# The u projection of each prompt tile as two column halves of the TensorE array

## What is computed

```python
h = rms_norm(x, norm1_g)
proj = h @ w_in
z, xbc, dt_raw, gu, gv = jnp.split(proj, ...)      # 512, 1024, 8, 512, 512 columns
...                                                # Mamba-2 scan over xbc and dt, gated by silu(z)
gu = jax.nn.gelu(gu)
gv = layer_norm(jax.nn.gelu(gv), ln_v_g, ln_v_b)
mixed = jnp.einsum("hts,bcshd->bcthd", w_s, v) + b_spatial...
gmlp_out = gu * mixed
x = x + jnp.concatenate([ssd_out, gmlp_out], axis=-1) @ w_out
x = x + hier_moe(rms_norm(x, norm2_g), ...)        # top 1 of 4 groups, top 2 of 8 experts
```

## Time and profile before

| | before |
|---|---|
| times of 3 runs | 2911.25 to 2912.52 us, median 2912.45 |
| the profiled execution: its time / its span | 2912.39 / 2910.5 us |
| TensorE busy | 2859.1 us, 98% of the span |
| TensorE weight loads busy | 1890.8 us, 65% |
| VectorE, ScalarE, GpSimd busy | 1580.8, 806.9, 878.5 us |
| the chain that ended last | TensorE 96% |
| granted TensorE clock, mean | 0.992 |

### The profile page before, as it was taken

How to read it: one execution, slowest core, us unless ns; L and a number is a source line. 1 busy time by engine, 2 the same in 40 slices (tenths; PEclk the granted TensorE clock), 3 DMA queues, 4 the chain that set the end, 5 groups by cost and what they waited for, 6 DMA issues and landing times.

```text
span 2910.5 us, 38335 instructions
## 1 busy us (share of the span) xinstructions
PE 2859.1 (98%) x12809; PEld 1890.8 (65%) x12809; DVE 1580.8 (54%) x4163; ACT 806.9 (28%) x1517; POOL 878.5 (30%) x1366
## 2 busy tenths in 40 slices
PE   8999999999999999999999999989999999999997
PEld 6677777677767776777777677754444444444443
DVE  5565555655565655565555656564444444444444
ACT  1223322323232323223222323212222222222222
POOL 0121112111211111121112111214566565666665
PEclk9999999999999999999999999989999999999999
DMA  7221221112121212211121112257675667567653
GB/s 312 106 79 52 73 80 52 59 66 80 52 71 60 74 51 73 74 58 59 66 80 51 61 64 73 75 220 250 246 261 186 221 202 257 202 220 265 245 169 126
DMA packets 109623, 369.01 MB, mean 127 GB/s; under 512 B 39497, under 2 KB 41426, under 8 KB 99442
## 3 DMA queue, kind: packets, MB, share of 16 engines
q1 hardware_dynamic: 48946, 252.91, 23.9%
q0 software_dynamic: 60480, 113.57, 11.8%
HBM read 325.09 MB, written 140.33 MB: 160 GB/s over the span
## 4 chain that ended last, share of the span: by engine, by line
PE 96%; DVE 2%; DMA 1%; issue 0%; POOL 0%; SPq 0%; ACT 0%; POOLq 0%; DVEq 0%; ACTq 0%
PE PB L368 23%; PE PB L1581 19%; PE PB L379 16%; PE PB L463 12%; PE SS L1621 9%; PE YB L463 4%; PE TB L1566 2%; PE YB L417 2%; PE TB L357 1%; DMA arena<-in_w_in 1%; PE SS L426 1%; PE TB L440 1%; PE SS L430 1%; PE TB L404 1%; PE YB L1614 1%; PE MB L408 1%
## 5 line engine op out<-in xcount | busy, mean ns | idle before, releaser
L368 PE MATMUL PB<-arena,hT 128*128 128x512 f32 (+2 forms) x2112 | 726.2, 497 | 1.2 <-DVE arena L1108 0.9
L368 PEld LDWEIGHTS PB<-arena,hT 128*128 128x128 f32 x2112 | 398.2, 191 | 269.4 <-issue 222.0
L1581 PE MATMUL PB<-arena,hT 128*128 x1296 | 569.3, 592 | 0.0
L379 PE MATMUL PB<-hT,arena 128*128 128x128 f32 x4224 | 487.8, 277 | 4.3 <-DVE arena L1096 4.3
L379 PEld LDWEIGHTS PB<-hT,arena 128*128 128x128 f32 x4224 | 482.3, 193 | 8.2 <-issue 4.6
L1581 PEld LDWEIGHTS PB<-arena,hT 128*128 128x128 f32 x1296 | 246.1, 190 | 309.7 <-issue 309.7
L1133 POOL TENSOR_SCALAR rs<-sq 128x2 f32<-128x2 f32 (+1 forms) x66 | 14.1, 214 | 1299.5 <-ACT h L732 960.8
L463 PE MATMUL PB<-arena,tT 128*128 128x274 f32 (+1 forms) x1056 | 358.7, 494 | 0.7 <-ACT tT L636 0.7
L1621 PE MATMUL SS<-arena,xdt 128*128 x640 | 287.9, 592 | 0.0
L463 PEld LDWEIGHTS PB<-arena,tT 128*128 128x128 f32 x1056 | 196.0, 190 | 141.3 <-issue 121.1
L795 DVE SCALAR_TENSOR_TENSOR xc<-xT,cols,xc 128x128 f32<-128x128 f32 x792 | 216.8, 346 | 3.5
(11 more groups left out here) (273 smaller groups left out, 3598.0 us busy)
## 6 DMA issues: line engine op xcount, KB each, us to landing
arena<-in_w_expert SPq DMA_DIRECT2D x32, 2048.0 KB, 8.8
arena<-in_w_expert SPq DMA_DIRECT2D x32, 1024.0 KB, 6.4
h_rows<-h SPq DMA_DIRECT2D x34, 512.0 KB, 2.7
x_in<-in_x_rows SPq DMA_DIRECT2D x33, 512.0 KB, 4.6
hT<-in_x_cols SPq DMA_DIRECT2D x33, 512.0 KB, 3.7
x_res<-in_x_rows SPq DMA_DIRECT2D x33, 512.0 KB, 5.1
dec<-running_sums SPq DMA_DIRECT2D x33, 512.0 KB, 3.6
first_rows<-bc SPq DMA_DIRECT2D x33, 512.0 KB, 4.0
```

Source lines behind the costliest of these rows:

```text
L368: mm = nc.tensor.matmul(out, hT[u][:, k, :], w_group(name)[:, k, :], start=k == 0, stop=k == KD - 1)
L379: mm = nc.tensor.matmul(PB[b][:, c * P:(c + 1) * P], w_block(name, c)[:, k, :], hT[u][:, k, :], start=k == 0, stop=k == KD - 1)
L1581: mm = nc.tensor.matmul(PB[u][:, :], hT[u][:, k, :], arena[:, bass.ds(slot + k * 2 * DE, 2 * DE)], start=k == 0, stop=k == KD - 1)
```

## The change

The u projection of the 32 tiles that `pe_turn` projects (tiles 1 to 32, the sample tile among them) is given as two matmuls for each `k`. One has the tokens 0 to 63 as its stationary operand and writes partitions 0 to 63 of `PB[0]`, the other has tokens 64 to 127 and partitions 64 to 127. Both have the same 512 moving columns of weights. Tile 0, projected in `pe_phase1`, stays as it was. The waits and the one semaphore increment, on the last matmul, stay.

```diff
+        def project_halves(pe, u, out, name, done, waits):
+
+            for sm, v in waits:
+                pe.wait_ge(s[sm], v)
+            for k in range(KD):
+                for r in (slice(0, P // 2), slice(P // 2, P)):
+                    mm = nc.tensor.matmul(out[r, :], hT[u][:, k, r], w_group(name)[:, k, :], start=k == 0, stop=k == KD - 1)
+            mm.then_inc(s[done], 1)
+
...
-            project(pe, v, PB[0][:, :], "u", "proj_u", [("xa_out", i + 2)])
+            project_halves(pe, v, PB[0], "u", "proj_u", [("xa_out", i + 2)])
```

## The result

The changed kernel takes 2922.93 us (median of 6 runs, 2921.16 to 2924.31) beside 2912.38 us for the kernel before in 6 runs: 10.55 us more, ratio 1.0037 with a 95% interval of 1.0024 to 1.0050. The profiled execution took 2923.50 us, 11.1 more than that of before. The forecast was 23 us more.

A forecast was written before the change was run, and what follows sets the result against it. The prediction took TensorE's stream to bound the kernel: 2912.4 us plus 13.7 for a 17th place in each projection plus 9.3 for switches gave 2935.4 us. Its own range was 2926 to 2949, the wider one 2920 to 3150.

The forecast's parts named there:

- TensorE alone sets the time: Tile turns: TensorE busy 1748.5 of 1753.0 us, so time added to its stream adds to the total.
- A record keeps its pace in part of the array: u projection: a 64-column record with 512 moving columns still takes 0.429 us.
- The halves overlap: u projection: records of the low and high token halves run at the same time; forecast chance 0.45.
- the largest rival: u projection: halves don't overlap, 16 more records, 7.16 us a projection with switches, 3141.5 us; chance 0.32.
- Late loads: u projection: halves overlap but each change of half shows a 64-column load, 0.86 us a projection, 2963 us; chance 0.13.
- If starts stay in program order ... 17 places of 0.429 us instead of 16: +0.43 us: u projection: low half's first record and high half's last run alone, the rest pair; 13.7 us for 32.
- The rival of separate queues: u projection: each half has its own queue, 16 places, and no switch cost; 2912.4 us, not slower; chance 0.10.
- the gaps at line 396 were no switch: Line 396, 8 stationary columns: its gaps are a semaphore wait, so the 0.29 us switch term falls.
- The switches: Around each u projection: array changes to 128*64 and back, 0.08 in, 0.10 out, 0.11 load; 0.29 us, 9.3 for 32.
- The upper bound of a whole tail and a whole load at each switch: Both switches around a u projection: 0.165 us tail plus 0.191 load each, 0.71 us a projection, 22.8 in all.
- The forecast's own 2926 to 2949 us: Whole kernel: range of the forecast case, paired halves with the lower and upper bounds of the switches.
- The wider one, 2920 to 3150: Whole kernel: range in us stretched to the case without overlap, leaving out some 0.15 of the chance.

The follow-up runs named there:

- blocks of eight: Changed kernel with the u projection as all eight low-half matmuls, then all eight high-half ones: 3083.46 us, ratio 1.0585 to the kernel before.
- two and four: Changed kernel with the halves of the u projection alternating every two k: 2923.52 us, ratio 1.0035; every four k: 2979.84 us, ratio 1.0232.

## Why the prediction was right and wrong

**TensorE alone sets the time: right.** TensorE's waits for other engines add up to 35 us before and after, within 1 us; 0.34 us a projection times 32 is the difference.

**A record keeps its pace in part of the array: right.** 0.429 us with 64 stationary columns, alone (blocks of eight), in pairs, or four at a time with 32.

**The halves overlap: right**, and the largest rival, single file at 3141.5 us, was wrong. Late loads (2963 us) were wrong too: from the second place on, the loads of both halves start with the pair ahead and are hidden.

**"If starts stay in program order ... 17 places of 0.429 us instead of 16: +0.43 us": this is the step that failed.** It was more than half of the sum, 13.7 of 23.0 us, and it is nothing. B's first record starts with A's first, ahead of A's second, which waits. Blocks of eight, two and four show how far that goes: the fourth waiting matmul record may start, the fifth may not. The rival of separate queues had the 16 places right and was given too little, though queues without a limit are not what blocks of eight show; its other half, that the gaps at line 396 were no switch, was wrong. The Trainium skill ("TensorE: Matmul & The Clock Gate", Part 3, "What overlaps and what doesn't") has matmuls start strictly in program order. Against the order of the code the runs disagree: B's first came three records early in blocks of eight. Its few ns between the starts of partners (Part 3, "Measured speedup vs the span model") agree with the trace: both starts fall in a window of 0.01 us.

**The switches: right in kind, a little small.** The term was 0.29 us a projection, measured 0.34. Way in 0.09 (0.08 taken), way out 0.10 (0.10), load of the next line 0.10 (0.11); the uncovered 64-column load of the first place, 0.05, was left out. The upper bound of a whole tail and a whole load at each switch (0.36) was far off. With 16 places and the forecast's own switch term the sum is 2912.4 + 9.3 = 2921.7 us, 1.2 under the median measured.

**The range.** The forecast's own 2926 to 2949 us missed the 2922.93 us. The wider one, 2920 to 3150, holds it, 3 us above its lower end, by its width and not by the mechanism that was forecast.

**What stays open.** The trace names no half in a record, so which half runs is worked out from counts. And the rows show the order of starts, not who makes it: a reach of TensorE over waiting records and a reordering of the same width ahead of the engine would look the same. The reach was measured with one kind of record alone, float32 with 512 moving columns.

## What to carry to other kernels

Column parts of the array run side by side at full pace each, so splitting a matmul whose moving columns set the pace gains nothing and costs a switch, about 0.35 us in and out here. Splitting one whose weight loads set the pace gains, because the loads run side by side too: 0.65 us of 1.73 here, 0.50 with the switches. Give the halves alternately, or at least within four waiting records of each other; and look for a small matmul with few stationary columns amid whole ones, since it pays for a switch that a wider operand avoids.

## What the hardware showed that was not expected

- A matmul record of one column part starts ahead of up to three waiting ones of another: 16, 16, 20 and 28 places of 0.429 us for blocks of 1, 2, 4 and 8.
- Weight loads of two column parts run at the same time: four loads of 64 columns in 0.20 us, 32 of them in 1.01 us where 16 of 128 columns took 1.94, and 32 records with 64 moving columns in 1.08 us where 16 of the whole array took 1.73.
- Four parts of 32 columns run at once as well as two of 64: 64 records in 7.00 us.
